# First attention of a two-block kernel with its fills reordered, and the causal mask of the second moved to TensorE

## The reference, cut to what matters

```python
def _diff_attn(q, k, v, lam):
    s = jnp.einsum("bqhcd,bkhcd->bhcqk", q, k) * (ATT_QK_DIM ** -0.5)   # c: two maps
    p = jax.nn.softmax(s, axis=-1)
    w = p[:, :, 0] - lam * p[:, :, 1]
    return jnp.einsum("bhqk,bkhd->bqhd", w, v)

def _long_conv(u, k2, bias):          # k2: the filter's taps, from a small sine network
    U, K = jnp.fft.rfft(u, n=2 * l, axis=1), jnp.fft.rfft(k2, axis=0)
    y = jnp.fft.irfft(U * K[None], n=2 * l, axis=1)[:, :l]
    return y + u * bias

# second block, one_block of the causal attention
s = jnp.where(k_idx[None, :] <= q_idx[:, None], s, -jnp.inf)
p = jax.nn.softmax(s, axis=-1)
```

## Time and profile before

| | |
|---|---|
| median of 3 executions | 2768.35 us (2765.82 to 2770.69) |
| the profiled execution | 2770.9 us, with a span of 2769.1 us |
| mean granted TensorE clock | 0.963 |
| busy in the span | PE 94%, PEld 70%, DVE 66%, ACT 34% |
| first attention, first scores to first product of `mixed[4]` | 224.4 to 456.7 us |
| second attention, layers 0 and 1 | 1491.7 to 1612.7 and 2221.6 to 2343.9 us |

### The profile page before, as it was taken

The page is one execution under the profiler, slowest core; times in us unless marked ns, Lnnn a source line. Parts: engine busy times, 40 slices in busy tenths (PEclk is TensorE's granted clock), DMA queues, the critical chain, the costliest instruction groups (busy, mean ns, idle before and its releaser), DMA issues.

```text
span 2769.1 us, 27674 instructions
## 1 busy us (share of the span) xinstructions
PE 2589.2 (94%) x10914; PEld 1951.4 (70%) x10914; DVE 1816.7 (66%) x2576; ACT 951.9 (34%) x1254; POOL 0.2 (0%) x4
## 2 busy tenths in 40 slices
PE   6997789999996699999999999999999998999997
PEld 4974335788885478888775477888877744788886
DVE  7886556866666875666997677565579865733334
ACT  4224332432321331333464333222235543432221
POOL 0000000000000000000000000000000000000000
PEclk8997899999998899999999989999999998999998
DMA  7351002345443145443221013454332210222322
GB/s 283 139 205 35 0 16 76 126 160 182 163 171 126 42 155 190 168 160 141 91 77 59 25 64 142 154 207 160 136 117 86 86 41 4 92 93 97 106 78 83
DMA packets 58249, 313.96 MB, mean 113 GB/s; under 512 B 6055, under 2 KB 11559, under 8 KB 37256
## 3 DMA queue, kind: packets, MB, share of 16 engines
q1 hardware_dynamic: 58120, 312.19, 31.4%
HBM read 310.07 MB, written 2.10 MB: 113 GB/s over the span
## 4 chain that ended last, share of the span: by engine, by line
PE 80%; DVE 15%; ACT 2%; DMA 1%; issue 1%; SPq 0%; DVEq 0%; ACTq 0%
PE psum L507 22%; PE psum L508 22%; PE psum L509 22%; PE psum L708 2%; PE psum L810 2%; DVE squares L1308 1%; DVE rstd L1260 1%; PE psum L555 1%; DVE x_lo L1303 1%; PE psum L829 1%; PE psum L838 1%; PE psum L828 1%; DVE w_lo L1409 1%; DVE ada_acc L1443 1%; DMA big<-in_ada 1%
## 5 line engine op out<-in xcount | busy, mean ns | idle before, releaser
L507 PE MATMUL psum<-x_hi,w_hi 128*128 128x512 f32 x1968 | 788.3, 401 | 13.5 <-DVE squares L1358 10.8
L508 PE MATMUL psum<-x_lo,w_hi 128*128 128x512 f32 x1968 | 770.6, 392 | 0.0
L509 PE MATMUL psum<-x_hi,w_lo 128*128 128x512 f32 x1968 | 770.0, 391 | 0.0
L1409 DVE TENSOR_TENSOR w_lo<-w_raw,w_hi 128x2048 fp32r<-128x2048 f32 (+1 forms) x192 | 418.6, 2180 | 283.4 <-ACT w_hi L955 281.4
L955 ACT ACTIVATE w_hi<-w_raw 128x2048 fp32r<-128x2048 f32 (+1 forms) x192 | 350.5, 1825 | 579.1 <-DMA w_raw<-in_w 564.9
L507 PEld LDWEIGHTS psum<-x_hi,w_hi 128*128 128x128 f32 x1968 | 372.3, 189 | 109.0 <-issue 23.1
L509 PEld LDWEIGHTS psum<-x_hi,w_lo 128*128 128x128 f32 x1968 | 371.8, 189 | 79.4
L508 PEld LDWEIGHTS psum<-x_lo,w_hi 128*128 128x128 f32 x1968 | 372.3, 189 | 78.3 <-issue 5.3
L507 PE MATMUL psum<-hidden_hi,w_hi 128*128 128x512 f32 x912 | 358.6, 393 | 0.0
L508 PE MATMUL psum<-hidden_lo,w_hi 128*128 128x512 f32 x912 | 355.1, 389 | 0.0
L509 PE MATMUL psum<-hidden_hi,w_lo 128*128 128x512 f32 x912 | 354.9, 389 | 0.0
(11 more groups left out here) (384 smaller groups left out, 2691.3 us busy)
## 6 DMA issues: line engine op xcount, KB each, us to landing
w_raw<-in_w SPq DMA_DIRECT2D x160, 1024.0 KB, 4.9
ada_w<-in_ada SPq DMA_DIRECT2D x116, 768.0 KB, 6.3
w_raw<-in_w SPq DMA_DIRECT2D x32, 704.0 KB, 4.1
big<-in_ada SPq DMA_DIRECT2D x12, 768.0 KB, 14.1
extra<-in_w_uq SPq DMA_DIRECT2D x8, 384.0 KB, 3.1
residual<-in_xT SPq DMA_DIRECT2D x2, 1024.0 KB, 9.5
small<-in_lru_w SPq DMA_DIRECT2D x2, 1024.0 KB, 7.0
out_xT<-residual SPq DMA_DIRECT2D x8, 256.0 KB, 2.1
```

The lines of the kernel that those rows point to most:

```text
L507: mm(o, w_h, x_h, start=first, stop=False)
L508: mm(o, w_h, x_l, start=False, stop=False)
L509: return mm(o, w_l, x_h, start=False, stop=last)
L1409: v.tensor_tensor(wl[:, r, 0:n], raw[:, r, 0:n], wh[:, r, 0:n].bitcast(f32), ALU.subtract).then_inc(w_split.sem, 1)
```

## The change

It computes the same. It does four things in the first attention and one in the second:

1. The first scores are issued before TensorE waits for the last short convolution, and DVE takes their maxima before that convolution. All of u is transposed at once after it, into banks 4 to 7, so that u's spectra fill steps 0 to 7; the taps take steps 4 to 9, the taps' spectra steps 10 to 14.
2. DVE reads the taps between `combine1(n)` and `max1(n + 1)`, not after the maxima.
3. `osum1` moves from before the transposes of its step to after fill b, and `oroot1` behind fill b on ACT; DVE's `head1` is cut in two, the reciprocal at step `q` = 2 and the rest at `q` = 3 of the next head, before the maxima.
4. All four `product(f)` and the low part of the next weight slot come before the last head's norm on DVE.
5. In the second attention the mask is added by TensorE, as one more matmul of the identity with the mask into the diagonal block; DVE's L1952 goes.

```diff
-        K_ORDER = ((11, 1, 0, 0), (12, 0, 1, 0), (13, 0, 0, 1), (13, 1, 1, 1), (14, 0, 0, 2), (14, 1, 1, 2),
-                   (15, 0, 0, 3), (15, 1, 1, 3))
+        TAP_STEPS = ((4, 0), (5, 0), (6, 0), (7, 0), (8, 0), (8, 1), (9, 0), (9, 1))
+        K_STEPS = ((10, 0), (10, 1), (11, 1), (12, 0), (12, 1), (13, 0), (13, 1), (14, 0))
...
-            a = {0: ("angle", 0), 1: ("turn", 1), 2: ("angle", 1)}.get(n)
-            b = {0: ("turn", 0), 1: ("turn", 2), 2: ("turn", 3), 12: ("last",)}.get(n)
...
+            a, b = {0: ("angle", 0), 2: ("angle", 1), 11: ("last",)}.get(n), None
+            uses = [a, ("u", n // 4, n % 4) if n < 8 else b]
+            for i, at in enumerate(TAP_STEPS):
+                if at[0] == n:
+                    uses[at[1]] = ("tap", i // 2, i % 2)
+            for i, at in enumerate(K_STEPS):
+                if at[0] == n:
+                    uses[at[1]] = ("k", i % 2, i // 2)
...
             def turn_u(j):
-                fill_free()
                 for t in range(4):
-                    ins = nc.tensor.transpose(ps[:, 7, t * P:(t + 1) * P], big[:, 20 + j, t * P:(t + 1) * P], ident[:])
-                filled(ins)
+                    ins = nc.tensor.transpose(ps[:, 4 + j, t * P:(t + 1) * P], big[:, 20 + j, t * P:(t + 1) * P], ident[:])
+                me.count(ins.then_inc(S("u_turns").sem, 1), S("u_turns"))
...
+            eng.wait_ge(staging_used.sem, mixed[3].staged0)
+            eng.wait_ge(evacuated.sem, mixed[4].evac0)
             scores1(0)
+            eng.wait_ge(S("proj1_ready").sem, S("proj1_ready").next(me))
+            for j in range(4):
+                turn_u(j)
             for n, (hd, q) in enumerate(steps1):
                 if n + 1 < len(steps1):
                     scores1(n + 1)
+                if n == 0:
+                    eng.wait_ge(S("u_turned").sem, 4)
+                fill(fill_of(n)[0])
                 if hd and q == 0:
                     values1(hd - 1)
-                fill(fill_of(n)[0])
-                if hd and q == 1:
-                    osum1()
                 eng.wait_ge(S("weights1").sem, S("weights1").next(me))
...
                 fill(fill_of(n)[1])
+                if hd and q == 1:
+                    osum1()
...
-                    mm(dst, qk[2][rows, q * P:keys], big[rows, 27, 0:keys], start=False, stop=True).then_inc(S("scores2").sem, 1)
+                    mm(dst, qk[2][rows, q * P:keys], big[rows, 27, 0:keys], start=False, stop=False)
+                    mm(ps[:, 2 + n % 3, q * P:keys], ident[:], causal[:], start=False, stop=True).then_inc(S("scores2").sem, 1)
...
             exps1(0)
+            for j in range(4):
+                eng.wait_ge(S("u_turns").sem, j + 1)
+                act(u_cols[:, :, j * P:(j + 1) * P], B(4 + j).rearrange("p (t n) -> p t n", n=P), ACT.Copy).then_inc(S("u_turned").sem, 1)
...
-                if hd and q == 1:
-                    oroot1(hd - 1)
                 fill(fill_of(n)[1])
                 if n in (0, 2):
                     sine(n // 2)
+                if hd and q == 1:
+                    oroot1(hd - 1)
...
                     dst = big[:, 16 + j, :] if j < 8 else t1[:]
+                    if j == 11:
+                        max1(0)
...
             def head1(hd):
-                inverse_root()
...
             for n, (hd, q) in enumerate(steps1):
                 combine1(n)
+                tap_of(fill_of(n)[0])
+                if hd and q == 3:
+                    head1(hd - 1)
                 if n + 1 < len(steps1):
                     max1(n + 1)
                 if n in (0, 2):
                     filter_angle(n // 2)
-                if 4 <= n < 12:
-                    tap_rows((n - 4) // 2, (n - 4) % 2)
                 if hd and q == 2:
-                    head1(hd - 1)
-            product(0)
-            product(1)
+                    inverse_root()
+                tap_of(fill_of(n)[1])
+            for f in range(4):
+                product(f)
+            split_lo(mixed[4].slot0)
+            inverse_root()
             head1(HEADS1 - 1)
-            product(2)
-            product(3)
-            split_lo(mixed[4].slot0)
             split_lo(mixed[4].slot0 + 1)
...
                     eng.wait_ge(S("scores2").sem, n + 1)
-                    diagonal = ps[:, 2 + c, q * P:(q + 1) * P]
-                    me.count(v.tensor_tensor(diagonal, diagonal, causal[:], ALU.add).then_inc(me.done.sem, 1), me.done)
-                    eng.wait_ge(*me.own())
```

More of the change, by code:

```diff
@@ L720, in fill @@
                     return
-                if use[0] == "turn":
-                    turn_u(use[1])
-                elif use[0] == "angle":
+                if use[0] == "angle":
                     filter_layer(use[1])
@@ L1091, in fill @@
                 eng.wait_ge(S("fill_out").sem, fill_at[use])
-                if use[0] == "turn":
-                    j = use[1]
-                    act(u_cols[:, :, j * P:(j + 1) * P], B(7).rearrange("p (t n) -> p t n", n=P), ACT.Copy).then_inc(S("fill_read").sem, 1)
-                    eng.wait_ge(S("fill_read").sem, fill_at[use])
-                    me.count(act(warm[:], eps5, ACT.Copy).then_inc(S("u_turned").sem, 1), S("u_turned"))
-                elif use[0] == "last":
+                if use[0] == "last":
                     act(k_spec[1][0][0:1, :], ps[0:1, 7, :], ACT.Copy, scale=V("dft_scale", p=1)).then_inc(S("fill_read").sem, 1)
@@ L1673, in _, with max1 @@
                 modulation(mixed[2], s)
+            def max1(n):
+                for c in range(2):
+                    at = 2 * (n % 2) + c
+                    eng.wait_ge(S("scores1").sem, S("scores1").next(me))
+                    me.count(v.reduce_max(rowmax[:, at:at + 1], ps[:, 2 * c:2 * c + 2, :].rearrange("p a t -> p (a t)")[:, 0:KEYS1], AX).then_inc(me.done.sem, 1), me.done)
+                    eng.wait_ge(*me.own())
+                    me.count(v.tensor_scalar(negmax[:, at:at + 1], rowmax[:, at:at + 1], -(64 ** -0.5), None, ALU.mult).then_inc(S("negmax1").sem, 1), S("negmax1"))
+                    eng.wait_ge(*me.own())
             for s in range(6):
@@ L1693, in _ @@
             eng.wait_ge(*me.own())
-            def max1(n):
-                for c in range(2):
-                    at = 2 * (n % 2) + c
-                    eng.wait_ge(S("scores1").sem, S("scores1").next(me))
-                    me.count(v.reduce_max(rowmax[:, at:at + 1], ps[:, 2 * c:2 * c + 2, :].rearrange("p a t -> p (a t)")[:, 0:KEYS1], AX).then_inc(me.done.sem, 1), me.done)
-                    eng.wait_ge(*me.own())
-                    me.count(v.tensor_scalar(negmax[:, at:at + 1], rowmax[:, at:at + 1], -(64 ** -0.5), None, ALU.mult).then_inc(S("negmax1").sem, 1), S("negmax1"))
-                    eng.wait_ge(*me.own())
             def combine1(n):
@@ L1775, in product, with tap_of @@
                 eng.wait_ge(*me.own())
-            max1(0)
+            def tap_of(use):
+                if use and use[0] == "tap":
+                    tap_rows(use[1], use[2])
             for n, (hd, q) in enumerate(steps1):
                 combine1(n)
+                tap_of(fill_of(n)[0])
+                if hd and q == 3:
+                    head1(hd - 1)
                 if n + 1 < len(steps1):
```

17 lines of the change are left out of this document (3 added, 14 removed).

## The result

The kernel after takes 2730.72 us (median of 4 executions, 2729.62 to 2732.06), the kernel before in the same comparison 2767.09 (4 executions, 2765.71 to 2770.69). The ratio is 0.9867, with a 95% interval of 0.985 to 0.9884. The forecast was 2748 in a range of 2733 to 2761: the sign is right, and the gain of 36.4 us lies just beyond the far end.

What follows compares the result with a forecast made beforehand. TensorE was taken as the bound, gaining only from idle time and half clock. 226.7 + 163.1 + 7.5 + 24.9 + 11.9 = 434.1 against 456.7 gains 22.6 us, less 2.7 for the mask: 2748, range 2733 to 2761.

Steps and rivals of the forecast that it cites:

- work at full clock behind it: First attention, after the last short convolution: TensorE's work without scores 0, 163.1 us, which the change can't shrink.
- The mask: Second attention: TensorE gains a 0.22 us matmul 64 times, DVE loses 0.31; both layers together some 2.7 us longer.
- The opening's half clock: Start of the first attention: TensorE at half clock until u's first two spectra have run, some 15 us; 7.5 lost.
- The waits: First attention, steps 0 to 15: TensorE's remaining waits sum to 24.9 us, where 41.7 of idle time were.
- The clock behind waits: First attention: seven waits of 1.5 us or more each cost 1.7 us at half clock, 11.9 in all.
- The signs: What would show it right: stage clock near 0.88, some 205 us from u's first spectrum to `mixed[4]`, second attentions 1 to 3 longer.
- The end: Last products of the first attention: `back(2)`'s 4.0 us wait goes, nothing replaces it; the last norm is covered by back matmuls.
- Rival 1: First attention: each of seven waits costs 3.4 us in clock, 11.9 more in all, 2760 us; chance 0.20.
- Rival 2: First attention: half-clock TensorE lets DVE catch up, so clock price and idle time aren't both paid; 2736 us; chance 0.12.
- Rival 3: Second attention: the mask on TensorE at 0.55 us in each of 64 steps costs 35.2 us; 2781 us; chance 0.04.
- Rival 4: First attention: handshakes only move, idle stays 41.7 us and clock 0.86; only the mask's cost is left; 2771; chance 0.03.
- Rival 5: ACT's table switches in the first attention: six each cost 1.28 us more, 7.7 in all; 2756 us; chance 0.01.

Runs made afterwards that it cites:

- none: Kernel before with the causal mask left out altogether, on DVE and on TensorE: 5.7 us less than the kernel before.
- late_open: Kernel after with the first scores and their maxima put back behind the last convolution, u still turned at once: 0.7 us more in the median than the kernel after.
- norm_only: Kernel before with only the norm's sum, root and cut head moved as in part 3: 17.2 us less than the kernel before.
- dve_mask: Kernel after with the mask put back on DVE: 4.7 us more in the median than the kernel after (1.6 told the other way).
- norm_last: Kernel before with the norm moved and all products ahead of the last head's norm (parts 3 and 4): 25.4 us less than the kernel before.
- best: Kernel after with norm's sum behind the next scores, taps and head's rest behind the maxima, head 2's norm between products, last values in bank 0: 2725.95 us.
- pe_only: Kernel before with part 5 alone, the mask added by TensorE and not by DVE: 7.5 us less than the kernel before.

## Why the forecast was right in sign and short in size

The parts measured singly are: norm 17.2, last products 8.5 and mask 7.5 (each alone on the kernel before), order of the fills 5.3, turning u at once 0.8, opening 0.7, taps -2.1. They sum to 37.9, against a measured 36.4. That it comes so near is in part luck, since three of the terms (order, opening, taps) can each be 3 us too large. By the stage lengths the parts of the first attention make 15.5 + 6.4 + 7.3 - 0.6 + 3.1 - 2.0 = 29.7 of 33.9 us, so some 4 us belong to no part alone. The mechanisms are those named, and additive within that. Against the forecast's sum, in the profiled executions:

```
term                                   forecast   measured
end of the last short convolution       226.7      227.2
work at full clock behind it            163.1      163.1 (taken)
half clock of the opening                 7.5        2.2
waits of TensorE                         24.9       20.9 (all idle time)
half clock behind the waits              11.9        9.9 (what is left)
first product of mixed[4]               434.1      423.3
both second attentions, change           +2.7       -7.3
```

- **The mask is the largest failed term, and of the wrong sign.** The step that failed is "Of the other 24, 8 stand beside those stretches of DVE and 16 on TensorE's path: 3.5 to 5.3 us". The pitch of 0.22 was right (0.23 net). What was wrong is that work on TensorE is paid at its own price. The layer ran at 0.91; with the mask on TensorE and DVE's addition gone it runs at 0.97, and the 7.4 us of new work a layer fit into 0.9 us more of busy time. The forecast had bounded it from below at "nothing, if all of it falls into the 10.7 of idle time", and never asked what the work does to the clock. The other side, DVE's 8 additions of 0.31, was forecast at 2.5 a layer and is 2.8 (5.7 / 2, from none). The sum also slipped here: 1.0 to 2.8 a layer are 2.0 to 5.6 for both, and the 2.7 that was taken is near their low end. The error is 10.0 of the 20.5 us by which the profiled execution (2730.47) lies under its forecast (2751.0), or 8.3 with the mean change of 5.6 over all the traces; the terms of the first attention make 10.8 more. The time lies 2.3 us below the range, so had the mask cost what was forecast it would lie inside.
- **The opening's half clock** was estimated to last until the first two spectra had run. It ended at 231.6, before the first of them. The 16 transposes behind the wait of 6.03, the scores and the network's layer keep TensorE without a gap from 227.22 to 234.7, and the clock rose in the midst of them. In late_open it rose 3.2 us behind the wait and fell again at 233.0; what decides that isn't shown. It is 5.3 us of the miss by the sum; late_open, with some 5 us of half clock in the same steps for 2.3, was 0.7 us longer in the median and 3.1 in its stage, so what it is worth there is less.
- **The waits** were mostly in the right places. Of the named ones, the norm's sum (3.2) and the last step (2.9 + 1.5) measure 3.27 and 3.00 + 0.96. The tap behind the root in step 6 (0.7) waited for nothing; a spectrum of a later head waited 0.61 for it. The angle's pair, which the sum counted once at 2.1 + 1.3 though the text has it in steps 0 and 2, came twice at 1.51 + 0.87; the three of 0.9 behind the reciprocal were one of 0.70; steps 9 and 10 gave 2.14 + 0.94 where 4.8 stood; scores 9 gave 2.31 for 3.4. 4.0 us of the miss.
- **The clock behind waits** was "seven at 1.7". Four waits behind the opening were followed by half clock: fewer than counted, and each dearer. The loss is 9.9 (2.5 each, 2.0 us of the miss) if the work is 163.1 us; counted in the trace it is 12.3 (3.1 each), and then this term was right in size by luck (four waits for seven) and 2.5 us of the miss stand in the work.
- **The signs.** The stage's clock was put near 0.88 and is 0.92, the 205 us from the first spectrum to `mixed[4]` are 187.1 (236.18 to 423.32), and the second attentions are shorter where they were to be longer.
- **The end** was right: no `back` waits, and the last norm is covered. Its last instruction on DVE starts at 412.32 and the back matmuls go on to 423.

**The rivals.** Rival 1 (waits breed half clock, 2760) did not happen in the time, though half clock did cost more per wait than the forecast had (2.5 to 3.1 for 1.7), and norm_only shows its ratio the other way round: 6.0 us of idle time removed gave back 9.4 in clock. Rival 2, a slower TensorE hiding waits, at 2736, came nearest to the time, but not by its mechanism: half clock and idle time were both paid. late_open shows the mechanism in part, in the opening alone (4.8 more busy, 1.8 less idle). Rival 3 (the mask as the bound) falls with the pitch of 0.23 and with the clock. Rival 4 falls with the 20.9 us idle. Rival 5: the loads of tables cost what they did, on ACT's timeline of step 5 of the kernel after, behind a wait for the norm's sum:

```profile
285.81 1.28 ACT L1085 ACT_TABLE_LOAD   x1 [2.26 <-PE psum L658]
287.11 0.69 ACT L1085 ACTIVATE rstd<-psum,cols 128x512 f32<-128x512 f32 x1
```

Load to root is 1.30 us, and the load starts as soon as the sum is there. The Trainium skill (ScalarE: Activation LUTs, What ACT_TABLE_LOAD costs) adds a drain of 1380 ns to a switch; neither this row nor that of before shows it.

**What stays open.** Why the norm gives 6.0 of idle time and 9.4 of clock on the kernel before, but 14.6 of idle time and 1.3 of busy time (176.55 for 175.22) on the kernel after, with stage lengths 15.5 and 15.9 apart, isn't explained. What in the mask's matmul lets the clock stay up, its presence in the gaps or the shorter idle time behind DVE's loss, is told apart only so far: DVE's addition gone without it gives 0.92, it with the addition kept 0.94 (0.96 in layer 1), both changes 0.97. Why a layer with DVE's mask can run at 0.90 in one trace and at 0.94 in another (dve_mask, norm_last), with the same idle time within 0.7 us, isn't shown either, so a part of the gain in a single pair of traces is chance. The differences of the single parts against the kernel after rest on another comparison's median, so those under 3 us can't be told from nothing.

## What to carry to other kernels

Where TensorE idles in pieces and its granted clock is below 1, count a stage's loss as idle time and half clock together, and read the clock of the stretch before pricing new TensorE work: work that fills gaps may cost nothing (the mask here), and an operation taken off the engine that answers each step (DVE here) is then a gain. Put a chain of several engines (sum, table load, root, reciprocal) behind the shared buffer's other users, so that nothing queues behind it, and put what the next stage waits for ahead of what it doesn't. Of the waits that can't be removed, it may pay to make the longest ones short: the best version has as much idle time as the kernel after in shorter pieces, and 2.8 us less of busy time.

## What the runs showed of the hardware

- TensorE got a higher clock for more work: layer 0 of the second attention ran at 0.92 with 346 matmul records (none) and at 0.97 with 409 (pe_only), in 117.9 and 117.8 us.
- The 128-row mask pair behind a 64-row one takes 0.42 us to the next start, and the projection behind it becomes 0.19 shorter (3.44 for 3.63): here the price of 128 rows behind 64 moved from the projection to the mask's pair.
- After 6.03 us of idle time TensorE ran at 0.50 for 4.4 us (227.2 to 231.6) and then at 0.99 and 1.00 for 35 us, though waits of 1.51 and 0.87 stand in them; after the waits of 3.27, 2.31, 2.14 and 3.00 it was at half clock again for a while, at 0.62 to 0.72 over the 9 to 12 us around each. In late_open it was at 0.50 from 233.0 to 239.8 with no wait over 0.54 us in the ten before.
- The same work got different clocks in different traces: a layer with DVE's mask is busy for 111.75 us at 0.90 in one (dve_mask, layer 0) and for 106.58 at 0.94 in another (norm_last, layer 1), with 10.7 and 11.4 us idle.
